# Half of each expert's down projection as three fp32r products, its weight parts made on GpSimd

## What is computed

```python
def expert_block(args):
    xb, e = args
    return (jax.nn.silu(xb @ w_gate[e]) * (xb @ w_up[e])) @ w_down[e]
...
y_rows = y_rows * row_w[:, None].astype(y_rows.dtype)
out = jnp.zeros((T + 1, D), y_rows.dtype).at[row_token].add(y_rows)[:T]
```

## Time and profile before

| | us |
|---|---|
| median of 3 runs | 869.8 |
| lowest and highest | 869.47, 870.5 |
| the profiled execution | 868.98 |
| its span in the trace | 867.2 |

### The profile page before, as it was taken

One profiled execution on the slowest core, in us unless ns is written; L12 is line 12 of the kernel. 1 busy time (PEld: TensorE's weight loads), 2 busy tenths in 40 slices (PEclk: granted clock), 3 DMA queues, 4 the chain that ended last, 5 costly groups with the idle time before them and its releaser, 6 DMA issues.

```text
span 867.2 us, 13148 instructions
## 1 busy us (share of the span) xinstructions
PE 813.8 (94%) x4792; PEld 660.9 (76%) x4792; DVE 523.7 (60%) x657; ACT 451.1 (52%) x590; POOL 125.7 (14%) x94
## 2 busy tenths in 40 slices
PE   6999999999999996998999989779999999999983
PEld 5888755999999994697899976467777777777761
DVE  3244435466556564655155565858888888888863
ACT  3243444454455443463244444267777777777741
POOL 0000001323422433103000000011111111111100
PEclk9999999999999998998799999889999999999996
DMA  9922221455555553152154543059999999999931
GB/s 368 386 98 97 97 97 48 150 192 194 193 172 179 185 190 103 43 190 102 50 195 146 194 149 143 0 197 351 369 353 378 373 352 353 380 359 373 373 146 50
DMA packets 25090, 181.44 MB, mean 209 GB/s; under 512 B 2784, under 2 KB 3040, under 8 KB 3296
## 3 DMA queue, kind: packets, MB, share of 16 engines
q1 hardware_dynamic: 25056, 180.97, 56.3%
HBM read 179.91 MB, written 1.05 MB: 209 GB/s over the span
## 4 chain that ended last, share of the span: by engine, by line
PE 86%; DVE 6%; ACT 3%; POOL 2%; issue 1%; DMA 1%; POOLq 0%; ACTq 0%; SPq 0%; DVEq 0%
PE psum L823 36%; PE psum L1032 15%; PE psum L1047 13%; PE psum L519 4%; PE psum L1053 3%; PE psum L618 3%; PE psum L527 2%; PE psum L577 1%; ACT junk L1145 1%; PE psum L1039 1%; PE psum L1024 1%; PE psum L942 1%; DVE arena L1764 1%; DVE ffn_w_low L438 1%; PE psum L940 1%
## 5 line engine op out<-in xcount | busy, mean ns | idle before, releaser
L438 DVE TENSOR_TENSOR ffn_w_low<-ring,ffn_w_high 128x2048 fp32r<-128x2048 f32 x57 | 135.0, 2372 | 123.4 <-ACT ffn_w_high L433 123.3
L433 ACT ACTIVATE ffn_w_high<-ring 128x2048 fp32r<-128x2048 f32 x57 | 109.2, 1918 | 144.1 <-PE psum L823 143.8
L823 PE MATMUL psum<-ht_high,ffn_w_high 128*128 128x256 f32 x576 | 164.3, 285 | 1.7 <-DVE ffn_w_low L438 1.1
L823 PE MATMUL psum<-ht_low,ffn_w_high 128*128 128x256 f32 x576 | 163.5, 284 | 0.0
L823 PE MATMUL psum<-ht_high,ffn_w_low 128*128 128x256 f32 x576 | 163.5, 284 | 0.0
L438 DVE TENSOR_TENSOR expert_w_low<-ring,expert_w_high 128x2048 fp32r<-128x2048 f32 x48 | 110.0, 2292 | 20.3 <-ACT expert_w_high L433 19.9
L1047 PE MATMUL psum<-ring,arena 128*128 128x512 f32 x256 | 116.7, 599 | 0.0
L823 PEld LDWEIGHTS psum<-ht_high,ffn_w_high 128*128 128x128 f32 x576 | 111.1, 193 | 3.2 <-issue 1.4
L1032 PE MATMUL psum<-expert_w_high,xw 128*128 128x256 f32 x384 | 106.1, 311 | 5.8 <-POOL xw L1543 3.9
L823 PEld LDWEIGHTS psum<-ht_low,ffn_w_high 128*128 128x128 f32 x576 | 111.1, 193 | 0.3
L823 PEld LDWEIGHTS psum<-ht_high,ffn_w_low 128*128 128x128 f32 x576 | 111.0, 193 | 0.0
(11 more groups left out here) (296 smaller groups left out, 1405.4 us busy)
## 6 DMA issues: line engine op xcount, KB each, us to landing
ring<-units_in SPq DMA_DIRECT2D x165, 1024.0 KB, 5.9
rows<-rows_in SPq DMA_DIRECT2D x1, 1688.0 KB, 12.3
arena<-bias_in SPq DMA_DIRECT2D x1, 1536.0 KB, 15.6
small<-small_in SPq DMA_DIRECT2D x1, 1232.0 KB, 25.5
const<-const_in SPq DMA_DIRECT2D x1, 1073.0 KB, 23.0
X<-x_in SPq DMA_DIRECT2D x1, 1024.0 KB, 4.9
out<-HN SPq DMA_DIRECT2D x2, 512.0 KB, 2.6
vec<-vec_in SPq DMA_DIRECT2D x1, 113.5 KB, 4.4
```

The costliest lines, as they stand in the source:

```text
L433: nc.scalar.activation(parts_slot(n)[0], w, ACT.Copy).then_inc(hi_ready, 1)
L438: nc.vector.tensor_tensor(l, ring[:, n % RING, :], h.bitcast(fp32), SUB).then_inc(lo_ready, 1)
L823: last = mm(o, l[a], r[b], start=start and (a, b) == pairs[0], stop=stop and (a, b) == pairs[-1])
```

## The change

For each expert, the product of the second half of the inner features (f = 1) stays fp32 and now comes first. The first half (f = 0) becomes three fp32r products for each half of the output: high times high, high activations times low weights, low activations times high weights.

- GpSimd makes the weight parts of the first 1024 columns of the down unit: `down_high` by multiplying them with a column of ones that is repeated, `down_low` by subtracting. There is one tile of each, so `split_down(e)` waits until TensorE has finished expert e-1's down projection, and it stands ahead of `window_lo(e+2)` in GpSimd's queue.
- ScalarE's one copy of the transposed activations becomes two, one to `ae_high` in fp32r and one to `AE` for f = 1.
- DVE makes `ae_low` from PSUM and `ae_high` (`turned_low`), between the low part of the gate unit and the sum of the halves.
- TensorE waits for `down_low` and `ae_low` behind the two fp32 products.
- `down_high` takes the space of `junk`, `down_low` that of `slot_onehot`; hence GpSimd's waits for `squares_summed` and `xs_done` ahead of the first expert.

```diff
+            def expert_down_parts(w, e, i):
+
+                for n in range(2):
+                    a = D + n * 512
+                    mm(psum[:, 2 + n, :], AE[:, 1, :], w[:, a:a + 512], start=True, stop=False)
+                pe.wait_ge(down_lo, i * 2 + (e + 1))
+                pe.wait_ge(ae_lo, i * 2 + (e + 1))
+                for n in range(2):
+                    for l, r in ((AEH, DH), (AEH, DL), (AEL, DH)):
+                        last = mm(psum[:, 2 + n, :], l[:, :], r[:, n * 512:(n + 1) * 512], start=False, stop=l is AEL)
+                return last
...
-                expert_down(w).then_inc(unit_used, 1)
+                expert_down_parts(w, e, i).then_inc(unit_used, 1)
...
-                copy(AE.rearrange("p f (d n) -> p f d n", d=2),
-                     psum[:, 1, 0:2 * CH].rearrange("p (f n) -> p f n", f=2).unsqueeze(2).to_broadcast([P, 2, 2, CH])
-                     ).then_inc(ae_ready, 1)
+                for f, dst in ((0, AEH[:, :]), (1, AE[:, 1, :])):
+                    last = copy(dst.rearrange("p (d n) -> p d n", d=2),
+                                psum[:, 1, f * CH:(f + 1) * CH].unsqueeze(1).to_broadcast([P, 2, CH]))
+                last.then_inc(ae_ready, 1)
...
+            def split_down(e, i=0):
+
+                w = unit(pool, down_of(e), i)[:, 0:D]
+                if e >= 1:
+                    pool.wait_ge(unit_used, i * RING + (down_of(e - 1) + 1))
+                nc.gpsimd.tensor_tensor(DH[:, :], w, ones[:, 0:1].to_broadcast([P, D]), MUL).then_inc(down_hi, 1)
+                pool.wait_ge(down_hi, i * 2 + (e + 1))
+                nc.gpsimd.tensor_tensor(DL[:, :], w, DH[:, :].bitcast(fp32), SUB).then_inc(down_lo, 1)
...
+            with pool.Fori(0, (EXPERTS - 6) // 2) as i:
+                for e in (4, 5):
+                    split_down(e, i)
+                    window_lo(e + 2, i)
...
+            def turned_low(e, i=0):
+                dve.wait_ge(ae_ready, i * 2 + (e + 1))
+                tt_op(AEL[:, :].rearrange("p (d n) -> p d n", d=2),
+                      psum[:, 1, 0:CH].unsqueeze(1).to_broadcast([P, 2, CH]),
+                      AEH[:, :].bitcast(fp32).rearrange("p (d n) -> p d n", d=2), SUB).then_inc(ae_lo, 1)
```

More of the change, by code:

```diff
@@ L176, in build @@
         XW = sb("xw", [P, 2, KD, 2 * CH], f32r)
-        junk = sb("junk", [P, D])
+        with nc.sbuf_tensor("junk", [P, D], fp32) as junk:
+            pass
+        DH = sb("down_high", [P, D], f32r)
+        AEH, AEL = (sb(f"ae_{part}", [P, 2 * CH], f32r) for part in ("high", "low"))
         RWH, RWL = (sb(f"rank_w_{part}", [P, KD * GLA_RANK], f32r) for part in ("high", "low"))
@@ L321, in build @@
                 pass
+            with nc.sbuf_tensor("down_low", [P, D], f32r) as DL:
+                pass
         PG = A.tile(TT, SLOTS)
@@ L374, in build @@
         y_hi, y_lo, scattered = map(sem, ("y_hi", "y_lo", "scattered"))
+        down_hi, down_lo, ae_lo = map(sem, ("down_hi", "down_lo", "ae_lo"))
         more_loaded, more_xw, more_up, more_silu, more_at, more_tr, more_ae, more_hi, more_lo, more_scattered = map(
@@ L1544, in window_lo @@
                                         SUB).then_inc(xw_lo, 1)
+            def split_down(e, i=0):
[5 more added lines that the diff above has]
+                nc.gpsimd.tensor_tensor(DL[:, :], w, DH[:, :].bitcast(fp32), SUB).then_inc(down_lo, 1)
             pool.wait_ge(starts_ready, 1)
+            for e in range(2):
+                window_lo(e)
+            pool.wait_ge(xs_done, KD)
+            pool.wait_ge(squares_summed, parts_before(11))
             for e in range(4):
[L1548 to L1551, removed]
+                split_down(e)
+                window_lo(e + 2)
+            with pool.Fori(0, (EXPERTS - 6) // 2) as i:
+                for e in (4, 5):
+                    split_down(e, i)
+                    window_lo(e + 2, i)
+            split_down(EXPERTS - 2)
+            split_down(EXPERTS - 1)
             for tt in range(TT):
@@ L2056, in experts @@
                     split_lo(dve, gate_of(e + 2), i)
+                turned_low(e, i)
                 if e < EXPERTS - 1:
```

## The result

The changed kernel took **948.8 us** (median of 4 runs, 948.6 to 949.4) against 869.8 before: a ratio of 1.0895, 95% interval 1.0862 to 1.0928. It is slower, as forecast, but by 79 us instead of 35, and outside the range of 882 to 932.

The account below looks back on a forecast made before the run. TensorE bound the expert phase at 8.62 us per expert; a shared DVE/GpSimd queue of 9.83 us would then bound it. 30 turns of +1.21 us (+36.3), less 0.5, on 868.98 gave 905 us, range 882 to 932.

Parts of the forecast that it names:

- TensorE: Down projection: six fp32r products replace two of four fp32 ones, saving 0.37 us per expert, leaving 8.25 us.
- The additions on ScalarE and DVE: Expert phase: ScalarE's second copy and DVE's 128x128 subtraction, some 0.3 us, costed at nothing because both engines have free time.
- The length of GpSimd's operations: down_high and down_low, 128x1024 each: 2.24 us apiece, range 1.89 to 2.58 us.
- The exclusion: DVE instructions with both inputs in SBUF and GpSimd instructions reading SBUF never run side by side; they share a port pair.
- a change of hands: Shared DVE/GpSimd port pair: the operation second in line saves about 0.14 us; six per expert save 0.84 us.
- The window part beside L2067: GpSimd's window part and DVE's results' low part, with one operand from PSUM, overlap and both keep their times.
- Rival (a): Expert phase: gaps of 0.3 to 1 us per turn in the shared queue add 9 to 30 us, 914 to 935; chance 0.10.
- the forecast's 9.83: Per-expert queue on the shared pair: DVE 4.99 plus GpSimd 5.68 less 0.84 us, against 8.62 us per turn before.
- L2085's growth: DVE's activation product: its time plus its wait was to grow most in relation, from 0.41 us.
- The clock: TensorE in the expert phase: a lower granted clock counts only in part, with 1.5 us of slack per turn.
- Rival (b): Pair does not serialise the new operations, as down_high's second operand is a repeated column; turn 8.28 us, 858 us; chance 0.11.

Follow-up runs that it names:

- the parts off: Changed kernel, but GpSimd's two weight-part operations shrink from 1024 columns to one after expert 0; 862.6 us, ratio 0.991 to the kernel before.

## Why the prediction was wrong

What held, by its own steps:

- **TensorE.** The six products take 1.39 us, forecast 1.40; the turn that this leaves is 8.30 us, forecast 8.25. I had bounded the saving by 0.31 and 0.45 and taken 0.37; it was the lower bound.
- **The additions on ScalarE and DVE** at nothing: with the parts off they cost nothing.
- **The length of GpSimd's operations.** For the last expert nothing disturbs them; GpSimd's timeline of the changed kernel there:

```profile
923.05 1.89 POOL L1570 TENSOR_TENSOR down_high<-ring,const 128x1024 fp32r<-128x1024 f32 x1 [5.97 <-PE psum L1065]
925.03 2.37 POOL L1572 TENSOR_TENSOR down_low<-ring,down_high 128x1024 fp32r<-128x1024 f32 x1
```

  1.89 and 2.37 us: the lower bound for the one with a repeated operand, between the bounds for the other, 2.13 on average where I had 2.24. One makes products and the other differences, so what of the 0.48 us is due to the repeated operand isn't shown. This would have made the time shorter, by 6 to 7 us.
- **The exclusion**, and the 0.14 us that a change of hands saves (L2085: 758.50 - 758.22 = 0.28 us behind down_high instead of 0.41).
- **The window part beside L2067**, each untouched.

The step that failed is the one from these pieces to the turn: "So the two engines' SBUF-to-SBUF operations form one queue", summed as if it were never empty. In the changed kernel the pair is idle from 750.68 to 751.06 and from 753.35 to 754.19, 1.2 us per turn, while DVE works off L2067, ae_low and the sum of the halves and GpSimd waits for TensorE. Rival (a) named such gaps, 0.3 to 1 us with a chance of 0.10, and even one of their conditions (down_high may not start before the last down projection is through), but not what keeps DVE off the pair meanwhile; the measured time lies above the end of its range, too.

The turn from one up part to the next (743.03 to 754.19, 11.16 us) adds up so: the forecast's 9.83, plus 1.22 in which the pair is idle, 0.14 for the one-hot rows' own share, and 0.19 since fewer changes of hands save time than the six reckoned with, less 0.22 for GpSimd's shorter operations.

Why the pair is idle goes back to a sentence before the sum: "A DVE operation that takes one operand from PSUM is not in this". It is right for L2031, on which it rested, but with it I had sorted the DVE instructions into those with two operands in SBUF and the harmless ones, and the one-hot rows were in neither list. No row of before shows them beside a GpSimd operation. They stand right behind the activation product and in front of L2067, so they pass the length of down_low on to L2067, which then comes to lie beside the window part instead. With them moved the idle time goes, and the shortest turns take 9.81 us. That this is the forecast's 9.83 to 0.02 us is in part luck: GpSimd's shorter operations would make it 9.61, and the one-hot rows, which the sum left out, hold the pair from 712.66 to 712.88, about 0.2 us.

In time, (11.21 - 9.83) x 30 = 41 us, and 2.9 us for the later start of the first down projection make the 44 us between 904.8 and 948.8. Of the 2.9, 1.8 are there before the stage begins: TensorE's products of L1030 end at 563.45 us, those of L1024 in before at 561.64. The run with the one-hot rows moved, which has the same instructions up to there, doesn't show them (561.60), so they aren't shown to be the change's; their cause is open. The rest is mainly the first activation product, 1.3 us instead of 0.4.

Of what was to show the forecast right, L2085's growth came out, and half of the rest: TensorE's idle time stood before the transposes, but also before the scatter; the chain was TensorE's to 52% of all and left it in the stage, but to DVE alone and not to GpSimd and DVE in turns. The DMA share fell to 0.76, not 0.83. DVE's weight parts did not grow (2.29 us), since they reached the pair first, and GpSimd's operations took 2.65 and 2.44 us, not 3 to 4: it was the short instructions of DVE that waited. The clock, part of rival (a), played next to no part: it was 1.00 from 640 to 900 us, and the 0.50 from 580 to 585 us made 14 up products of the first turn 0.4 us longer (3.30 us against 2.87 before). Rival (b), that the repeated operand escapes, is refuted by L2085 behind down_high.

## What to carry to other kernels

A resource that two in-order engines exclude each other from is not costed by the sum of its busy times alone: lay both queues side by side in time, and ask of every instruction that stands behind a held-up one whether it could have run meanwhile. A short instruction can carry a long wait, so each form on the engine needs its own row, or counts as unknown. The same weight parts cost 79 us in one arrangement and gained 7 in another. Giving the high part to ScalarE was not enough (908 us); the low part had to be put where DVE was idle or read from PSUM, with a second tile for the high part (863 us).

## What the runs showed of the hardware

- A GpSimd `tensor_tensor` of 128x1024 fp32 took 1.89 us as a product with a repeated column, 2.37 us as a difference of two tiles; a memset of 128x1023 took 0.96 us.
- A DVE `tensor_scalar` of 128x256 from SBUF to SBUF (0.34 us alone) waits for a running GpSimd operation, whether that reads (2.46 us) or only writes (0.83 us); a DVE `tensor_tensor` with both operands in SBUF waits for the reading one (2.11 against 0.41 us) and not for the writing one (0.41 us). DVE's `scalar_tensor_tensor` with one operand in PSUM took its normal 1.29 us beside both.
- Held up, an instruction shows as busy: DVE's 99% in this stage holds 3.6 us per turn of waiting in two instructions (2.00 - 0.41 and 2.33 - 0.34 us). No wait row names it; only two mean times of one form, or the other engine's timeline, do.
